# One transformer pair on one core: stick-breaking sums from rounded log rows and their rests, the output gate copied by ScalarE, few-row products placed among other products, and another bank pair for one query unit

## The chip, the core and the metric

The kernel runs on one core of one Trainium2 chip. The metric is the device time of one execution in microseconds (us), lower is better. The program is one stream of instructions for each engine: TensorE (PE, with its weight loads shown apart as PEld), VectorE (DVE), ScalarE (ACT), GpSimd (POOL) and SyncE (SP, which issues the loads). Engines meet only at semaphores that the kernel sets and waits on by hand.

## The reference, cut to what matters

Two blocks run one after the other on x of 256 tokens by 1024 features, all in float32. The first block mixes a stick-breaking attention (8 heads of 64) with a recurrent RWKV-7 layer (8 heads of 64), gates and adds them, and ends in a gated feed-forward part. The second block has dilated attention with a short convolution, a cross-attention to a memory of 256 rows, and a squared-ReLU feed-forward part. Two pieces of the first block bear on the change:

```
kk = k * k_k                                   # per head
kk = kk / max(norm(kk), 1e-12)                 # squares gathered over 64 features, root spread back
g  = sigmoid(xg) @ g_up                        # output gate of the recurrent layer
y  = groupnorm(scan) * lnx_w + lnx_b
out_rw = (y + bonus) * g                       # needs g * lnx_w and (bonus + lnx_b) * g

z  = q @ k.T                                   # stick-breaking attention, key j < query t
log_beta, log_rest = log_sigmoid(z), log_sigmoid(-z)
w[t, j] = exp(log_beta[t, j] + sum(log_rest[t, i] for j < i < t))
```

The sum over i is a product with a triangular matrix of ones, computed on TensorE on top of the logits in the same banks of PSUM.

## The kernel before, in words

All weights arrive in units of 1 MB (128 partitions by 2048 float32, names `raw`, `whi`, `wlo`), in a ring of three. SyncE loads a unit, ScalarE rounds it to float32r (`hi`, line 1289), VectorE subtracts to get the rest (`lo`, line 1762), and TensorE multiplies by activations that are split in the same way (`xhl`, rounded `xh` and rest `xl`). A product of float32r operands is one instruction; a product of plain float32 operands shows as two. A unit of 256 columns in `by_feature_wide` (line 519) is, for each of two tiles of 128 features, eight products of 512 columns by `whi` and eight of 256 columns by `wlo`; the function takes a hook `amidst(f, k)` that is called ahead of each product of 512 columns.

The order of the first block on TensorE is written by hand. Seven units `U_RW` (index 0 to 6) give the inputs of the recurrent layer, by `by_feature`; four units `U_QK` give queries and keys; two `U_V` give values; eight `U_G` give the gates. Placed among them:

- behind unit 4 of `U_RW` (line 664): the gather of squares `kq`, four products that give 8 rows (`kk_ss`). ScalarE takes the root (`krs`, `kk_sd`, line 1387); VectorE clips it and takes the reciprocal (lines 1850 and 1851, `kk_rs`), in its queue behind the evacuation of unit 5 and the rest `lo` of unit 8.
- behind the first unit of `U_QK` (line 680): the spread of `krs`, four products out of 8 rows (`kk_spread`), which wait for `kk_rs`.
- behind the first unit of `U_V` (line 689): the gate product with `gup` into banks 4 and 5 and the bonus sums into banks 6 and 7 (`bonus_mm`). VectorE reads all four banks (lines 1894 to 1905) and sets `gn_pre`. TensorE waits for `gn_pre` at line 851, before the stick-breaking logits of the first head pair overwrite banks 4 and 5.

Then a loop over four head pairs `p_` (line 862). Each turn: the logits into banks 4 and 5 (`sb_z`), a gate unit, the triangular sums (`sb_arg`), a second gate unit, the product with the values (`sb_o`). Inside and behind the gate units lie the small products of the recurrent layer (`before`, `amid`, `behind`): among them `join(i)`, which waits for VectorE's `Gm`, and, for the first pair, `before(1)`, which waits for VectorE's `Tm` (`pair_ready` 3). For a pair ScalarE makes `st1 = ln(1 + exp(-|z|))` in three steps, VectorE makes `st2` in two (lines 1970 and 1971, `sb_lf`), and the sums are float32 products of the constants `tri` (384 columns, two of them) and `ones` (128 columns, two) with `st2`. VectorE then makes `st3` (line 1978), ScalarE the exponential `st4`.

In the second block, lines 1067 to 1078 run four units `U_QK2`. Before them the memory's keys lie in banks 0 and 1 (`km`): ScalarE copies a half out, VectorE adds the other (line 1767, `summed`). Unit 0 uses bank 6, unit 1 uses banks 0 and 1 and so waits for that sum, unit 2 uses banks 6 and 7, unit 3 banks 0 and 1. After it comes a value unit in banks 2 and 3.

Of the kernel before, what the change touches and what calls it, by code (L numbers as in the profile page):

```python
# [6 lines left out]
P = 128  # L7
# [79 lines left out]
def block_kernel(nc, A, out, dbg=None):  # L87
# [9 lines left out]
    with ctx:  # L97
# [46 lines left out]
        st4 = at("st4", W + 91, [P, 2, 384])  # L144
        lora = at("lora", W + 94, [P, HW])
# [207 lines left out]
        QK2_BANKS = (None, (0, 1), (6, 7), (0, 1))  # L353
# [87 lines left out]
        def _(pe):  # L441
# [217 lines left out]

            for i, u in enumerate(U_RW):  # L660
                if i >= 3:
                    pe.wait_ge(sem("out_evac"), i - 2)
                by_feature(u, xh, xl, RW_BANK[i], None if i else "n1", amid_first(i))
                if i == 4:

                    pe.wait_ge(sem("kk_sq"), 1)
                    pe.wait_ge(sem("lora_evac"), 1)
                    pe.wait_ge(sem("cst_loaded"), 16)
                    for j in range(NPAIR):
                        last = mm(PS[0:NH, 4 * 512:4 * 512 + SEQ], C("gather")[:, NH * j:NH * (j + 1)], kq[:, j, :], j == 0,  # L670
                                  j == NPAIR - 1)
                    last.then_inc(sem("kk_ss"), 1)

            for i, u in enumerate(U_QK):
                if i == 1:
                    pe.wait_ge(sem("out_evac"), 7)
                elif i >= 2:
                    pe.wait_ge(sem("summed"), halved("qk", i - 1))
                by_feature_wide(u, xhl, QK_BANKS[i % 2])
                if i == 0:  # L680

                    pe.wait_ge(sem("kk_rs"), 1)
                    for j in range(NPAIR):
                        last = mm(PS[:, 4 * 512 + j * SEQ:4 * 512 + (j + 1) * SEQ], C("spread")[0:NH, j * P:(j + 1) * P], krs[:],
                                  True, True)
                    last.then_inc(sem("kk_spread"), 1)
# [113 lines left out]
            def amid(i):  # L800
# [13 lines left out]
                else:  # L814
                    pe.wait_ge(sem("chunk_ready"), 3)
                    tokens(eN, 0, "tok_T")
                    pe.wait_ge(sem("sb_arg_read"), NPAIR)
# [33 lines left out]
            pe.wait_ge(sem("gn_pre"), 1)  # L851
            def gate_unit(i):
# [9 lines left out]
            for p_ in range(NPAIR):  # L862

                if p_ == 0:
                    pe.wait_ge(sem("out_evac"), 11)
                else:
                    pe.wait_ge(sem("sb_arg_read"), p_)
# [5 lines left out]
                last.then_inc(sem("sb_z"), 1)  # L873
# [10 lines left out]
                pe.wait_ge(sem("sb_w"), p_ + 1)  # L884
# [9 lines left out]
                last.then_inc(sem("sb_o"), 1)  # L894
# [172 lines left out]
            for i, u in enumerate(U_QK2):  # L1067
# [4 lines left out]
                if i == 1:  # L1072
                    pe.wait_ge(sem("summed"), halved("km", 2))
                elif i == 2:
                    pe.wait_ge(sem("out2_evac"), 1)
                else:
                    pe.wait_ge(sem("summed"), halved("qk2", 1))
                by_feature_wide(u, xhl, QK2_BANKS[i])
            by_token(U_V2[0], xh, xl, 0, 2, True, False)

            def dilated_logits(p_):
# [3 lines left out]
                else:  # L1085
                    pe.wait_ge(sem("d_z_read"), p_)
# [4 lines left out]
                last.then_inc(sem("d_z"), 1)  # L1091
# [11 lines left out]
            def dilated_values(p_):  # L1103
# [7 lines left out]
                last.then_inc(sem("d_o"), 1)  # L1111
# [155 lines left out]
        def _(act):  # L1267
# [126 lines left out]
            A_(eX[:], sg[:], ACT.Exp, scale=-c0).then_inc(sem("decays"), 1)  # L1394
            for i, u in enumerate(U_QK):
# [3 lines left out]
            hi(U_V[0] + RING)  # L1399
            after(U_V[1])  # L1400
# [26 lines left out]
            for p_ in range(NPAIR):  # L1427
                act.wait_ge(sem("sb_z"), p_ + 1)
# [7 lines left out]
                if p_:  # L1436
                    hi(U_G[2 * p_ - 1] + RING)
                if p_:
# [9 lines left out]
                act.wait_ge(sem("sb_arg_read"), p_ + 1)  # L1448
                if p_:
                    act.wait_ge(sem("sb_o"), p_)  # L1450
                A_(st4[:], st3[:], ACT.Exp).then_inc(sem("sb_w"), 1)
# [12 lines left out]
            act.wait_ge(sem("sb_o"), NPAIR)  # L1464
# [120 lines left out]
            def dilated_exp(p_):  # L1585
# [5 lines left out]
                last.then_inc(sem("d_p"), 1)  # L1591
# [16 lines left out]
            for p_ in range(NPAIR):  # L1608
# [7 lines left out]
                if p_:  # L1616
                    act.wait_ge(sem("d_o"), p_)
# [14 lines left out]
            act.wait_ge(sem("d_o"), NPAIR)  # L1632
# [114 lines left out]
        def _(dve):  # L1747
# [147 lines left out]
            dve.wait_ge(sem("rw_pre"), 1)  # L1895
            for j in range(NPAIR):
                V.tensor_scalar(rw[:, j, :], PS[:, 4 * 512 + j * SEQ:4 * 512 + (j + 1) * SEQ], par_col("lnx_w", j), None, ALU.mult)
# [3 lines left out]
            link(last)  # L1901
            for j in range(NPAIR):
                last = V.scalar_tensor_tensor(out=rw[:, 4 + j, :], in0=bon[:, j, :], scalar=par_col("lnx_b", j),
                                              in1=PS[:, 4 * 512 + j * SEQ:4 * 512 + (j + 1) * SEQ], op0=ALU.add, op1=ALU.mult)
            last.then_inc(sem("gn_pre"), 1)
# [37 lines left out]
            def gate_unit(i):  # L1943
# [19 lines left out]
            for p_ in range(NPAIR):  # L1963
# [7 lines left out]
                V.tensor_tensor(st2[:], st2[:], M("sb_neg").unsqueeze(1).broadcast_to([P, 2, 384]), ALU.mult).then_inc(sem("sb_lf"), 1)  # L1971
# [4 lines left out]
                if p_:  # L1976
                    dve.wait_ge(sem("sb_w"), p_)
# [441 lines left out]
```

## Time and profile before

| | us |
|---|---|
| median of 3 runs | 841.4 (840.96 to 841.78) |
| the profiled execution | 841.16 |
| its span, first to last instruction | 839.4 |
| around the span | 1.8 |

| engine | busy us | share of the span | instructions |
|---|---|---|---|
| PE | 824.6 | 98% | 6332 |
| PEld | 715.2 | 85% | 6332 |
| DVE | 586.9 | 70% | 693 |
| ACT | 430.8 | 51% | 529 |
| POOL | 6.4 | 1% | 8 |

The mean granted clock of TensorE is 0.997 of full speed. The profile has several views. The page sums up one execution. The waits list who waited for whom. The timeline gives instructions of one engine in order of time; a row can merge several alike. A row's length reaches to the end of the last result, while the next product has already begun, so what a product costs is read from the starts of rows that follow each other. The windows give busy time and granted clock of a stretch. The groups by form give the count and cost of instructions of one shape.

### The profile page before, as it was taken

The page shows a single profiled execution, that of the slowest core. Times are in us where ns is not written, and L with a number is a line of the kernel's source. Part 1 is how long each engine was busy: PE and PEld are TensorE (multiplying, and loading weights), DVE is VectorE, ACT ScalarE, POOL GpSimd, SP SyncE. Part 2 cuts the span into 40 slices and gives each one's busy share as a digit, 9 for nine tenths or more (in the row PEclk, how much of TensorE's full clock was granted, in tenths as well). Part 3 has the DMA queues.
Part 4 walks back from the last instruction along what each step waited for, and adds up shares of the span by engine and source line. Part 5 has one row for each costly group of instructions (what it writes and reads, how often), then busy time and mean ns, then how long its engine had stood idle before and what let it go on. Part 6 is the DMA issues. An engine that isn't in the chain of part 4 may idle for free.

```text
span 839.4 us, 14921 instructions
## 1 busy us (share of the span) xinstructions
PE 824.6 (98%) x6332; PEld 715.2 (85%) x6332; DVE 586.9 (70%) x693; ACT 430.8 (51%) x529; POOL 6.4 (1%) x8
## 2 busy tenths in 40 slices
PE   9999999999999999999998999999999999999997
PEld 9998788888989888888887888888888888888885
DVE  5999865656887666656678567795764866676664
ACT  6644344474387544544466365546654544444443
POOL 0000010000000000000000000000000000000000
PEclk9999999999999999999999999999999999999999
DMA  9845513331764555565545553546423365555541
GB/s 301 289 152 177 175 53 102 103 102 52 280 209 159 180 201 185 165 216 185 200 157 177 168 194 108 192 143 201 167 100 126 133 228 182 180 180 183 192 149 50
DMA packets 96999, 140.55 MB, mean 167 GB/s; under 512 B 2480, under 2 KB 79408, under 8 KB 96944
## 3 DMA queue, kind: packets, MB, share of 16 engines
q1 hardware_dynamic: 96512, 139.36, 49.7%
q8 instruction: 43, 0.70, 0.3%
q10 hardware_dynamic: 432, 0.39, 0.2%
q14 instruction: 12, 0.10, 0.0%
HBM read 138.69 MB, written 1.05 MB: 166 GB/s over the span
## 4 chain that ended last, share of the span: by engine, by line
PE 83%; DVE 10%; ACT 3%; issue 3%; DMA 1%; POOL 0%; ACTq 0%; DVEq 0%; POOLq 0%
PE PS L443 81%; DVE wlo L1762 3%; ACT whi L1271 1%; PE PS L569 1%; DMA raw<-in_w_in_dram 1%; ACT st L1271 1%; DVE rw L1828 1%; ACT xhl L1271 1%; DVE diff L1825 1%; DVE stg L1823 1%; PE PS L1100 0%; DVE cs L1845 0%; PE PS L716 0%; DVE xhl L1789 0%; DVE TT L1924 0%
## 5 line engine op out<-in xcount | busy, mean ns | idle before, releaser
L1762 DVE TENSOR_TENSOR wlo<-raw,whi 128x2048 fp32r<-128x2048 f32 x122 | 278.2, 2289 | 78.7 <-ACT whi L1271 78.5
L443 PE MATMUL PS<-xhl,whi 128*128 128x512 f32 (+1 forms) x1328 | 308.5, 365 | 3.9 <-DVE km L1767 2.9
L1271 ACT ACTIVATE whi<-raw 128x2048 fp32r<-128x2048 f32 (+1 forms) x130 | 241.3, 1859 | 93.6 <-PE PS L443 90.1
L443 PEld LDWEIGHTS PS<-xhl,whi 128*128 128x128 f32 x1328 | 230.3, 190 | 40.3 <-DVE km L1767 3.1
L443 PE MATMUL PS<-xhl,wlo 128*128 128x256 f32 x1136 | 180.3, 282 | 0.1
L443 PEld LDWEIGHTS PS<-xhl,wlo 128*128 128x128 f32 x1136 | 163.7, 191 | 9.7 <-DVE wlo L1803 0.3
L443 PE MATMUL PS<-whi,fh 128*128 128x512 f32 x216 | 84.3, 391 | 0.0
L443 PE MATMUL PS<-wlo,fh 128*128 128x512 f32 x216 | 84.3, 390 | 0.0
L443 PE MATMUL PS<-whi,fl 128*128 128x512 f32 x216 | 84.0, 389 | 0.0
L1767 DVE TENSOR_TENSOR fa<-PS,fa 128x512 f32<-128x512 f32 x25 | 17.3, 691 | 62.7 <-ACT fa L1271 62.7
L443 PEld LDWEIGHTS PS<-whi,fl 128*128 128x128 f32 x216 | 40.6, 188 | 8.6
L443 PEld LDWEIGHTS PS<-whi,fh 128*128 128x128 f32 x216 | 40.7, 188 | 7.8
L443 PEld LDWEIGHTS PS<-wlo,fh 128*128 128x128 f32 x216 | 40.7, 188 | 7.5
L1271 ACT ACTIVATE fa<-PS 128x512 f32<-128x512 f32 x25 | 14.7, 589 | 52.4 <-PE PS L443 52.4
L1789 DVE SCALAR_TENSOR_TENSOR xhl<-PS,par,xhl 128x256 fp32r<-128x256 f32 x40 | 16.7, 476 | 11.7 <-ACT xhl L1271 11.7
L1271 ACT ACTIVATE fh<-fa 128x512 fp32r<-128x512 f32 x16 | 10.1, 633 | 25.9 <-DVE fa L2357 25.9
L1271 ACT ACTIVATE xhl<-PS,par 128x256 fp32r<-128x256 f32 x40 | 15.7, 481 | 12.1 <-PE PS L569 12.1
L443 PE MATMUL PS<-whi,memhl 128*128 128x512 f32 x64 | 20.7, 397 | 0.1
L443 PE MATMUL PS<-whi,xhl 128*128 128x512 f32 x64 | 20.7, 394 | 0.0
L1271 ACT ACTIVATE fh<-fb 128x512 fp32r<-128x512 f32 x11 | 7.0, 632 | 24.9 <-DVE fb L2173 24.9
L1271 ACT ACTIVATE gates<-PS 128x512 f32<-128x512 f32 x8 | 4.8, 597 | 27.9 <-PE PS L443 27.9
L1271 ACT ACTIVATE junk<-xres 128x1024 f32<-128x1024 f32 (+1 forms) x14 | 13.2, 945 | 9.9 <-DVE xres L2116 8.7
(327 smaller groups left out, 1035.3 us busy)
## 6 DMA issues: line engine op xcount, KB each, us to landing
raw<-in_w_in_dram SPq DMA_DIRECT2D x32, 1024.0 KB, 5.3
raw<-in_w_up_dram SPq DMA_DIRECT2D x16, 1024.0 KB, 5.3
raw<-in_w_down_dram SPq DMA_DIRECT2D x16, 1024.0 KB, 5.1
raw<-in_w_ffn_gate_dram SPq DMA_DIRECT2D x11, 1024.0 KB, 5.3
raw<-in_w_ffn_up_dram SPq DMA_DIRECT2D x11, 1024.0 KB, 5.3
raw<-in_w_ffn_down_dram SPq DMA_DIRECT2D x11, 1024.0 KB, 5.6
raw<-in_w_kv_mem_dram SPq DMA_DIRECT2D x8, 1024.0 KB, 5.3
raw<-in_w_o_dram SPq DMA_DIRECT2D x4, 1024.0 KB, 8.2
```

Source lines behind the costliest of these rows:

```text
L443: return nc.tensor.matmul(o, l, r, start=start, stop=stop, **kw)
L569: last = nc.tensor.transpose(PS[:, o:o + P], src[:, t, f * P:(f + 1) * P], C("ident"))
L1271: return nc.scalar.activation(o, i, f, **kw)
L1762: V.tensor_tensor(wlo[u % RING][:], raw[u % RING][:], whi[u % RING][:].bitcast(f32), ALU.subtract) \
L1767: return V.tensor_tensor(dst, tiles(banks)[:, :, 0], dst, ALU.add)
L1789: V.scalar_tensor_tensor(out=lo_[:, f0 + f, :], in0=PS[:, b * 512 + c * SEQ:b * 512 + (c + 1) * SEQ], scalar=par_col(g, f), in1=hi_[:, f0 ...
L1823: V.tensor_tensor(s[:, :, 1:SEQ + 1], two(RW_BANK[i]), spread(rs1[:]), ALU.mult).then_inc(sem("out_evac"), 1)
L1825: link(V.tensor_tensor(diff[:], s[:, :, 0:SEQ], s[:, :, 1:SEQ + 1], ALU.subtract))
L1828: last = V.scalar_tensor_tensor(out=rw[:, r, :], in0=diff[:, f, :], scalar=par_col("mu_rw", r), in1=s[:, f, 1:SEQ + 1], op0=ALU.mult, op1= ...
```

## The change

Five edits:

- Triangular sums: `st2` (the masked log rows) is rounded to float32r by ScalarE (`lfh`, in the place of `st3`), VectorE takes the rest (`lfl`, in the place of `st2`), and the sums are float32r products of rounded `tri_r` and `ones_r` with both parts. VectorE's subtraction stands in `gate_unit` behind `lower_out`, ahead of the wait for the gate's second half. `tri_r` and `ones_r` are made once by ScalarE.
- Output gate: ScalarE copies banks 4 and 5 out, once scaled by `lnx_w`, once plain into `rw[:, 4:8]` (`g_read`), and VectorE's product with the gate reads that. TensorE waits for `gn_pre`, now set behind VectorE's read of banks 6 and 7, and for `g_read`.
- The four gather products stand one by one in unit 5 of `U_RW`, two steps of `k` apart; the four spread products one by one in unit 0 of `U_QK`, at `k` of 2 and 6 of either tile. The wait for `kk_rs` goes with the first of them.
- Unit 1 of `U_QK2` uses banks 2 and 3; the wait for the sum of the memory's keys goes to unit 3, and the value unit waits for the sum of unit 1.
- Semaphores of the two attention parts are shared (`logits`, `logits_read`, `pair_weights`, `pair_values`), with counts carried on.

```diff
-        QK2_BANKS = (None, (0, 1), (6, 7), (0, 1))
+        QK2_BANKS = (None, (2, 3), (6, 7), (0, 1))
...
+            def gather_squares(f, k):
+
+                if f or k % 2:
+                    return
+                j = k // 2
+                if j == 0:
+                    pe.wait_ge(sem("kk_sq"), 1)
+                    pe.wait_ge(sem("lora_evac"), 1)
+                    pe.wait_ge(sem("cst_loaded"), 16)
+                last = mm(PS[0:NH, 4 * 512:4 * 512 + SEQ], C("gather")[:, NH * j:NH * (j + 1)], kq[:, j, :], j == 0, j == NPAIR - 1)
+                if j == NPAIR - 1:
+                    last.then_inc(sem("kk_ss"), 1)
+
+            def spread_norms(f, k):
+
+                if k not in (2, 6):
+                    return
+                j = 2 * f + k // 4
+                if j == 0:
+                    pe.wait_ge(sem("kk_rs"), 1)
+                last = mm(PS[:, 4 * 512 + j * SEQ:4 * 512 + (j + 1) * SEQ], C("spread")[0:NH, j * P:(j + 1) * P], krs[:], True, True)
+                if j == NPAIR - 1:
+                    last.then_inc(sem("kk_spread"), 1)
...
-                by_feature(u, xh, xl, RW_BANK[i], None if i else "n1", amid_first(i))
+                by_feature(u, xh, xl, RW_BANK[i], None if i else "n1", amid_first(i), 0, gather_squares if i == 5 else None)
...
-                by_feature_wide(u, xhl, QK_BANKS[i % 2])
+                by_feature_wide(u, xhl, QK_BANKS[i % 2], amidst=None if i else spread_norms)
...
             pe.wait_ge(sem("gn_pre"), 1)
+            pe.wait_ge(sem("g_read"), 1)
...
-                for e in range(2):
-                    mm(PS[:, (4 + e) * 512:(4 + e) * 512 + 384], C("tri"), st2[:, e, :], False, False, skip_group_check=True)
-                for e in range(2):
-                    last = mm(PS[:, (4 + e) * 512 + P:(4 + e) * 512 + SEQ], C("ones"), st2[:, e, SEQ:384], False, True, skip_group_check=True)
+                for part in (lfh, lfl):
+                    for e in range(2):
+                        mm(PS[:, (4 + e) * 512:(4 + e) * 512 + 384], tri_r[:], part[:, e, :], False, False, skip_group_check=True)
+                for part in (lfh, lfl):
+                    for e in range(2):
+                        last = mm(PS[:, (4 + e) * 512 + P:(4 + e) * 512 + SEQ], ones_r[:], part[:, e, SEQ:384], False, part is lfl,
+                                  skip_group_check=True)
...
-                if i == 1:
-                    pe.wait_ge(sem("summed"), halved("km", 2))
-                elif i == 2:
-                    pe.wait_ge(sem("out2_evac"), 1)
-                else:
-                    pe.wait_ge(sem("summed"), halved("qk2", 1))
+                if i == 2:
+                    pe.wait_ge(sem("out2_evac"), 1)
+                elif i == 3:
+                    pe.wait_ge(sem("summed"), halved("km", 2))
                 by_feature_wide(u, xhl, QK2_BANKS[i])
+            pe.wait_ge(sem("summed"), halved("qk2", 1))
             by_token(U_V2[0], xh, xl, 0, 2, True, False)
...
+            act.wait_ge(sem("bonus_mm"), 1)
+            act.wait_ge(sem("rw_pre"), 1)
+            for j in range(NPAIR):
+                A_(rw[:, j, :], PS[:, 4 * 512 + j * SEQ:4 * 512 + (j + 1) * SEQ], ACT.Copy, scale=par_col("lnx_w", j))
+            for j in range(2):
+                last = A_(rw[:, 4 + 2 * j:6 + 2 * j, :], bank(4 + j).rearrange("p (j t) -> p j t", j=2), ACT.Copy)
+            last.then_inc(sem("g_read"), 1)
...
+                act.wait_ge(sem("sb_masked"), p_ + 1)
+                A_(lfh[:], st2[:], ACT.Copy).then_inc(sem("sb_hi"), 1)
...
+                if i % 2 == 0:
+                    dve.wait_ge(sem("sb_hi"), i // 2 + 1)
+                    dve.wait_ge(sem("sb_masked"), i // 2 + 1)
+                    V.tensor_tensor(lfl[:], st2[:], lfh[:].bitcast(f32), ALU.subtract).then_inc(sem("sb_lf"), 1)
```

## Rows read from the trace of the kernel before

**Rows 1.** The page: busy time of each engine.

```profile
PE 824.6 (98%) x6332; PEld 715.2 (85%) x6332; DVE 586.9 (70%) x693; ACT 430.8 (51%) x529; POOL 6.4 (1%) x8
```

**Rows 2.** The waits of PE: who, for whom, us in total, times, longest.

```profile
PE PS L443 <- DVE km L1767: 2.9, 1, 2.9
PE PS L443 <- DVE rw L1903: 1.8, 1, 1.8
...
PE PS L443 <- DVE sq L1767: 0.2, 1, 0.2
```

**Rows 3.** Timeline of PE, first unit of `U_QK`, the spread: start, length, shape, count.

```profile
53.21 2.00 PE L443 MATMUL PS<-xhl,whi 128*128 128x512 f32 x8
55.05 1.12 PE L443 MATMUL PS<-xhl,wlo 128*128 128x256 f32 x8
...
58.89 1.99 PE L443 MATMUL PS<-krs,cst 8*128 8x256 f32 x8
60.91 0.50 PE L443 MATMUL PS<-xhl,whi 128*128 128x512 f32 x1
```

**Rows 4.** Timeline of DVE in the same stretch.

```profile
53.21 2.28 DVE L1762 TENSOR_TENSOR wlo<-raw,whi 128x2048 fp32r<-128x2048 f32 x1
...
55.72 1.74 DVE L1851 RECIPROCAL krs<-krs 8x256 f32<-8x256 f32 x1
```

**Rows 5.** Timeline of PE, the gate and bonus products.

```profile
83.69 1.89 PE L443 MATMUL PS<-rw,gup 128*128 128x256 f32 x8
85.41 1.89 PE L443 MATMUL PS<-rkk,cst 128*128 128x256 f32 x8
```

**Rows 6.** Windows: length, busy of PE, PEld, DVE, ACT, POOL; granted clock, DMA.

```profile
92.70:94.50 1.80, 0.05 (x1) 0.00 (x0) 1.71 (x5) 1.65 (x1) 0.00 (x0) 1.00 1.09 346
...
457.80:458.70 0.90, 0.00 (x0) 0.00 (x0) 0.90 (x3) 0.22 (x1) 0.00 (x0) 0.97 1.02 398
458.70:461.70 3.00, 2.96 (x7) 2.38 (x8) 2.78 (x2) 0.00 (x0) 0.00 (x0) 0.50 0.83 243
```

**Rows 7.** Timeline of DVE, then of ACT, around the gate product's evacuation.

```profile
85.50 4.49 DVE L1762 TENSOR_TENSOR wlo<-raw,whi 128x2048 fp32r<-128x2048 f32 x2
91.48 1.28 DVE L1899 TENSOR_TENSOR bon<-PS,rw 128x512 f32<-128x512 f32 x2
92.85 1.91 ACT L1271 ACTIVATE whi<-raw 128x2048 fp32r<-128x2048 f32 x1 [7.00 <-PE PS L443]
```

**Rows 8.** Timeline of PE, then of DVE, first head pair.

```profile
104.46 2.00 PE L443 MATMUL PS<-st,cst 128*128 128x384 f32 x8
106.30 0.60 PE L716 MATMUL PS<-cst,eX 128*128 128x128 f32 x4
106.83 1.09 PE L443 MATMUL PS<-cst,eX 128*64 128x128 f32 x16
...
102.64 1.28 DVE L1912 TENSOR_TENSOR TT<-PS,msk 128x512 f32<-128x512 f32 x2
104.71 1.28 DVE L1912 TENSOR_TENSOR Tm<-PS,msk 128x512 f32<-128x512 f32 x2
```

**Rows 9.** Timeline of PE, then of DVE and ACT, second head pair.

```profile
128.49 1.90 PE L443 MATMUL PS<-st,cst 128*128 128x384 f32 x8
130.14 0.48 PE L443 MATMUL PS<-xhl,whi 128*128 128x512 f32 x1
...
126.13 0.74 DVE L1931 TENSOR_TENSOR Gm<-PS,msk 128x256 f32<-128x256 f32 x2
119.64 1.72 ACT L1271 ACTIVATE st<-st 128x768 f32<-128x768 f32 x2
```

**Rows 10.** Timeline of PE, second block, after unit 0 of `U_QK2`; then DVE.

```profile
458.74 3.63 PE L443 MATMUL PS<-xhl,whi 128*128 128x512 f32 x8 [2.94 <-DVE km L1767]
462.21 1.11 PE L443 MATMUL PS<-xhl,wlo 128*128 128x256 f32 x8
...
452.15 2.29 DVE L1762 TENSOR_TENSOR wlo<-raw,whi 128x2048 fp32r<-128x2048 f32 x1 [0.76 <-ACT whi L1271]
```

More of the change, by code:

```diff
@@ L662, in _ @@
                     pe.wait_ge(sem("out_evac"), i - 2)
-                by_feature(u, xh, xl, RW_BANK[i], None if i else "n1", amid_first(i))
[L664 to L672, printed above, removed]
+                by_feature(u, xh, xl, RW_BANK[i], None if i else "n1", amid_first(i), 0, gather_squares if i == 5 else None)
             for i, u in enumerate(U_QK):
@@ L678, in _ @@
                     pe.wait_ge(sem("summed"), halved("qk", i - 1))
-                by_feature_wide(u, xhl, QK_BANKS[i % 2])
[L680 to L686, printed above, removed]
+                by_feature_wide(u, xhl, QK_BANKS[i % 2], amidst=None if i else spread_norms)
             for i, u in enumerate(U_V):
@@ L893, in _ @@
                     last = mm(PS[half(e), ob + P:ob + SEQ], sv[:, 1, head(2 * p_ + e)], st4[:, e, SEQ:384], False, True, skip_group_check=True)
-                last.then_inc(sem("sb_o"), 1)
+                last.then_inc(sem("pair_values"), 1)
             def place(g):
@@ L1090, in dilated_logits @@
                     last = mm(PS[:, (4 + e) * 512 + P:(4 + e) * 512 + 384], q2[half(e), p_, P:SEQ], k2[half(e), p_, :], True, True)
-                last.then_inc(sem("d_z"), 1)
+                last.then_inc(sem("logits"), 1)
             def dilated_turn(p_):
@@ L1110, in dilated_values @@
                     last = mm(PS[half(e), o + P:o + SEQ], v2[:, 1, head(2 * p_ + e)], dq[:, e, SEQ:384], False, True, skip_group_check=True)
-                last.then_inc(sem("d_o"), 1)
+                last.then_inc(sem("pair_values"), 1)
             def dilated_fill(i):
@@ L1427, in _ @@
             for p_ in range(NPAIR):
-                act.wait_ge(sem("sb_z"), p_ + 1)
+                act.wait_ge(sem("logits"), p_ + 1)
                 if p_:
@@ L1590, in dilated_exp @@
                                   accum_out=col(DL + 4 * p_ + 2 * t + e))
-                last.then_inc(sem("d_p"), 1)
+                last.then_inc(sem("pair_weights"), 1)
             def fill_tile(i, f):
@@ L1900, in _ @@
                                        rw[:, 8 + 2 * j:10 + 2 * j, :], ALU.mult)
-            link(last)
+            last.then_inc(sem("gn_pre"), 1)
+            dve.wait_ge(sem("gn_pre"), 1)
+            dve.wait_ge(sem("g_read"), 1)
             for j in range(NPAIR):
                 last = V.scalar_tensor_tensor(out=rw[:, 4 + j, :], in0=bon[:, j, :], scalar=par_col("lnx_b", j),
-                                              in1=PS[:, 4 * 512 + j * SEQ:4 * 512 + (j + 1) * SEQ], op0=ALU.add, op1=ALU.mult)
-            last.then_inc(sem("gn_pre"), 1)
+                                              in1=rw[:, 4 + j, :], op0=ALU.add, op1=ALU.mult)
+            link(last)
             lo(U_V[1] + RING)
@@ L2213, in dilated_max @@
                 z = PS[:, 4 * 512:6 * 512].rearrange("p (e n) -> p e n", e=2)[:, :, 0:384]
-                dve.wait_ge(sem("d_z"), p_ + 1)
+                dve.wait_ge(sem("logits"), NPAIR + p_ + 1)
                 if p_:
-                    dve.wait_ge(sem("d_p"), p_)
+                    dve.wait_ge(sem("pair_weights"), NPAIR + p_)
                 V.scalar_tensor_tensor(out=dz[:], in0=z, scalar=HD ** -0.5, in1=C("dil").unsqueeze(1).broadcast_to([P, 2, 384]),
-                                       op0=ALU.mult, op1=ALU.add).then_inc(sem("d_z_read"), 1)
-                dve.wait_ge(sem("d_z_read"), p_ + 1)
+                                       op0=ALU.mult, op1=ALU.add).then_inc(sem("logits_read"), 1)
+                dve.wait_ge(sem("logits_read"), NPAIR + p_ + 1)
                 for t, r in enumerate((slice(0, P), slice(P, 384))):
```

40 lines of the change are left out of this document (22 added, 18 removed).

## The prediction

> **What bounds the kernel now.** I read the page first: TensorE is busy in 98% of the span, VectorE in 70%, ScalarE in 51% [rows 1]. So time is won or lost where TensorE does less, stands still or runs slower. The waits of PE come next, since they say how little standing still there is: the longest are 2.9 us for the sum of the memory's keys, 1.8 us for the last product of the gate's evacuation, and 0.2 us for the first query sum [rows 2]. The change goes at the first two. The reader should then open the timelines of PE and of DVE side by side at each edit. From 53 to 58 us VectorE works without a gap [rows 4], while TensorE runs ahead of it; whatever makes TensorE ask for a VectorE result earlier there turns this lead into a wait. The windows with the granted clock come last. They show one fall: TensorE stands for 2.9 us until 458.74, and from 458.70 on it is granted 0.50 of full speed, its level of 1.2 GHz, before it is back at 2.4 GHz. The stand of 1.8 us before 94.50 was followed by no fall [rows 6].
>
> **Second block, banks 2 and 3 for unit 1.** The wait of 2.9 us falls away [rows 10]. Its eight products of 512 columns took 3.47 us (458.74 to 462.21) where the same eight take 1.84 us at full clock (53.21 to 55.05) [rows 3, 10], so the fall cost 1.63 us, and it goes with the stand that came before it. What is late next? Unit 1's rest was made from 452.15 to 454.4, before TensorE is free at 455.8 [rows 10]. The sum that unit 3 now waits for was ready at 458.7, and unit 3 starts two units of 5.6 us later. The value unit waits for a sum that is more than ten us old. Gain 4.6 us; bounds 4.2 and 4.8.
>
> **The spread, moved forward.** This is the term that speaks against the change. Before, the spread began at 58.89, behind the whole unit [rows 3], and nothing was waited for. Now its first product, and with it the wait for `kk_rs`, stands behind two products of 512 columns of that unit, which begins at 53.21: 2 x 0.23 = 0.46 us in, so at 53.7. The reciprocal ends at 55.72 + 1.74 = 57.46 [rows 4]. VectorE has no gap ahead of it and loses no work there, so it comes no sooner. All of TensorE's queue stands behind this wait. The gather, placed apart in a unit before, makes TensorE some 0.6 us later; that falls into the stand and costs nothing, but without it the stand is 3.8 us instead of 3.2. From 57.5 on the rest of the unit runs, 5.6 - 0.46 = 5.13 us, and with it the spread. Together in one run the spread takes 2.0 us (58.89 to 60.91) [rows 3]. A run of the same size with full weights takes 1.72 us (83.69 to 85.41) [rows 5]; the difference of 0.3 us is what going into and out of a product of 8 rows costs. Four such goings in place of one would add 0.9 us, nothing at the least (1.7 in all), 1.4 at the most. I take 2.9 us, nearest to the rows of this very product. So the next unit starts at 57.5 + 5.13 + 2.9 = 65.5 where it started at 60.91 [rows 3]: 4.6 us later (3.4 to 5.1). Two waits behind it are absorbed, the 0.2 us and the 1.8 us [rows 2]. Left: +2.6 us (1.4 to 3.1).
>
> Rule and row agree here in direction, and the rule goes against this edit. The Trainium skill, "TensorEngine Tiling (Array Packing)", section Key Properties, says that changing the tiling mode drains the engine; by it each of the four goings pays, and this sum would be at its upper end, 0.5 us more. Whether a product of 8 rows is another mode here, no row says.
>
> **The clock behind that stand.** TensorE stands for 3.2 to 3.8 us, longer than the 2.9 us after which the clock fell, and nearly twice the 1.8 us after which it did not [rows 6, 10]. I take it that the clock falls again and costs what it cost there: 1.6 us (0 if it does not fall, 1.7 at most).
>
> **The output gate by ScalarE.** VectorE is at `lo` until 85.50 + 4.49 = 89.99, then its two products `bon` take 1.3 us, so `gn_pre` is set at 91.3 instead of 94.5 [rows 7]. ScalarE stood idle for 7.0 us before 92.85 [rows 7]; six copies of no more than 0.86 us each, the price of a 768-column copy [rows 9], are 5.2 us at most and begin when the bonus sums end, at 85.41 + 1.72 = 87.1 [rows 5]. `g_read` is then there before TensorE ends the value unit at 92.7, and that order stays when TensorE is 4.6 us late. This removes the 1.8 us, which is already taken off above. VectorE's other products with the gate come later and delay only a rest that waits for ScalarE anyway.
>
> **Triangular sums.** Before, a pair's sums take 1.84 us (104.46 to 106.30) and 1.65 us (128.49 to 130.14), 1.75 us in the mean [rows 8, 9]. After, they are eight instructions of float32r: four of 384 columns and four of 128. One of 512 columns takes 0.23 us; one of 256 takes (58.89 - 53.21 - 16 x 0.23) / 16 = 0.12 us [rows 3]; so 384 take 0.175, four 0.70 us. No float32r product of 128 columns is in the trace. The low bound is half of 0.12; the high bound is all that a float32 product of 128 columns costs, two instructions of 0.13 us (106.30 to 106.83 for four) [rows 8]. I take one instruction of that, 0.13, the nearest in shape: 0.5 us. That is 1.2 us a pair (0.95 to 1.75), a gain of 0.55 us.
>
> ScalarE's rounding of `st2` adds 0.86 us [rows 9] and VectorE's rest 0.95 us a pair. In the second pair VectorE ends `Gm` at 126.87 and would end the rest at 127.8; TensorE wants it at 128.49 [rows 9]. It is covered with 0.7 us to spare, and the later pairs have the same order. In the first pair it is not: `TT` ends at 103.9 [rows 8], the rest at 104.9, and TensorE wants it at 104.46. Queued behind it on VectorE are the gate's sum (0.65 us) and `Tm` (1.25 us), which TensorE needs next. So `Tm` ends at 106.8, where TensorE was free at 106.30 [rows 8]: +0.5 us in the first pair, its gain swallowed (0.3 to 1.0). Three pairs gain 3 x 0.55 = 1.7 us (0 to 2.4). The two rounded constants cost ScalarE about half a us while TensorE stands. The shared semaphores keep the order of the waits and cost nothing.
>
> **The sum.** 2.6 + 1.6 + 0.5 - 1.7 - 4.6 = -1.6 us on the profiled execution of 841.16, which is 839.6 us. That execution is 0.24 us below the median of 841.4, too little to shift it. Elsewhere TensorE is without waits worth naming [rows 2], so a us that it gains or loses arrives at the end.
>
> **Rivals.**
> - The clock does not fall in the stand. For it: the one fall came when TensorE had stood for 2.9 us, little less than here, and one case makes no law. Against: this stand is longer. The 1.6 us go: 838.0 us.
> - The short float32r products are slow or the rests come late, so the pairs give nothing: 839.6 + 1.7 = 841.3 us. For it: no row has such a product, and the cover of the rest is 0.7 us. Against: the wide float32r products are paid by the column.
> - Slower: the clock stays low after the stand, because the spread's products, which use 8 of 128 rows, stand among the others for the whole unit. Work left in that unit is 8.0 us; at half the clock throughout it costs 8.0 instead of 1.6 us more, so 839.6 + 6.4 = 846.0 us. It decides the sign once the low clock costs over 1.6 + 1.8 + 1.7 = 5.1 us. Against: after 458.70 full clock was back in some three us [rows 6], and the spread run of before saw no fall. The Trainium skill, "TensorE: Matmul & The Clock Gate", section What's actually happening, calls the throttled level the default and says activity releases it; how a product of 8 rows counts as activity it does not say.
> - The change does not do what it says: the stand does not arise because `kk_rs` comes at 53.7. It would need VectorE to skip 3.8 us of queue; nothing does that. It would give 839.6 - 1.6 - 3.2 = 834.8 us.
>
> **How the numbers follow.** Chances: forecast 0.50, no fall 0.28, pairs give nothing 0.12, slower 0.07, no stand 0.03. The forecast's own range, from its bounds, is 838.2 to 841.0. The range of 8 in 10 takes in the no-fall case with the pairs and the second block at their good bounds (836.6) and the pairs giving nothing (841.3). About 0.2%, 1.7 us, is what a measurement of this kernel can tell from no change, so faster means below 839.7. The forecast falls there in a bit over half its cases (0.27), the no-fall case nearly always (0.27), the last one too (0.03): 0.57. Slower means above 843.1: 0.07 and a rest of mishaps, 0.08. The same: 0.35.
>
> **What would show it.** In the profile of after: a wait of PE for `krs` (line of the reciprocal) of 3.2 to 3.8 us near 57.5, and a granted clock of 0.50 behind it; no wait for `km`, and full clock in the second block; no wait at the first logits; sums of a pair within 1.2 us; a short wait of PE for `Tm` in the first pair. I am wrong by 3 us if the stand is not there, by 1.6 if the clock stays up, by up to 1.7 if a pair's sums take as long as before.

## The result, and the profile after

| | before | after |
|---|---|---|
| median, us | 841.35 (6 runs, 840.96 to 841.78) | 844.95 (6 runs, 840.75 to 845.68) |
| profiled execution, us | 841.16 | 845.28 |
| its span, us | 839.4 | 843.5 |
| mean granted clock in it | 0.997 | 0.989 |

The ratio is 1.0037, with a 95% interval of 1.0023 to 1.005: slower by 0.4%, where 839.6 was forecast and 841.3 was the upper end of the range. The executions of the changed kernel mostly fall in two groups, near 841 and near 845.4, and the mean granted clock goes with them (0.994 and 0.989), so below a time is read beside its clock. By 843 us times a difference in mean clock one gets roughly the time that the clock took: 0.005 is 4 us. It is rough because a low clock behind TensorE's last product costs nothing: in a kernel below (the spread back in its old place) such a tail of 2.9 us is nearly all that is missing from 1.00, and the mean is 0.998.

The page of the changed kernel. Its first row answers to [rows 1]; the second is TensorE's granted clock in 40 slices of 21 us, in tenths.

```profile
PE 830.3 (98%) x6332; PEld 718.2 (85%) x6332; DVE 588.6 (70%) x693; ACT 436.9 (52%) x541; POOL 7.0 (1%) x8
PEclk9987999999999999999999999999999999999999
```

TensorE has as many instructions as before and is busy 5.7 us longer. The clock row says where to look: the third and fourth slices, 42 to 84 us.

The waits of PE in the changed kernel, as in [rows 2].

```profile
PE PS L448 <- DVE krs L1879: 2.7, 1, 2.7
...
PE PS L729 <- DVE Tm L1940: 0.4, 1, 0.4
...
PE PS L448 <- DVE lfl L1984: 0.3, 1, 0.3
```

The two long waits of before are gone, `km` and the last product of the gate's evacuation. One of 2.7 us has come for the reciprocal, and two short ones in the first head pair.

The timeline of PE in the changed kernel, first unit of `U_QK` with the spread in it (start, length, operation, shape, count, idle time before), as in [rows 3].

```profile
54.14 0.63 PE L448 MATMUL PS<-xhl,whi 128*128 128x512 f32 x2
57.49 1.22 PE L448 MATMUL PS<-krs,cst 8*128 8x256 f32 x2 [2.72 <-DVE krs L1879]
58.63 2.08 PE L448 MATMUL PS<-xhl,whi 128*128 128x512 f32 x4
60.64 1.22 PE L448 MATMUL PS<-krs,cst 8*128 8x256 f32 x2
61.79 1.22 PE L448 MATMUL PS<-xhl,whi 128*128 128x512 f32 x2
...
65.50 1.22 PE L448 MATMUL PS<-krs,cst 8*128 8x256 f32 x2
...
68.65 1.22 PE L448 MATMUL PS<-krs,cst 8*128 8x256 f32 x2
...
72.53 2.95 PE L448 MATMUL PS<-xhl,whi 128*128 128x512 f32 x8
```

The windows of the changed kernel over the same stretch (length; busy of PE, PEld, DVE, ACT, POOL; granted clock; DMA).

```profile
53.00:57.50 4.50, 1.78 (x14) 1.35 (x13) 4.46 (x5) 3.08 (x2) 0.00 (x0) 1.00 0.18 25
57.50:72.00 14.50, 14.50 (x36) 9.17 (x37) 8.55 (x17) 3.46 (x6) 0.00 (x0) 0.50 0.38 137
72.00:74.00 2.00, 2.00 (x8) 1.71 (x8) 0.60 (x1) 1.23 (x2) 0.00 (x0) 0.50 0.00 0
74.00:76.00 2.00, 2.00 (x12) 1.72 (x11) 1.58 (x3) 1.17 (x1) 0.00 (x0) 0.86 0.04 8
```

Four products of 512 columns take 2.01 us (58.63 to 60.64) where they take 0.92 us at full clock. The clock is at 0.50, its level of 1.2 GHz, from 57.5 until about 74.5: of the last window 28% is still low. That is 17 us, over the whole rest of this unit and the start of the next. The next unit begins at 72.53 instead of 60.91 [rows 3].

The other edits, in the changed kernel. The timeline of PE at the sums of the first and the second head pair, as in [rows 8, 9].

```profile
115.04 0.62 PE L448 MATMUL PS<-lfh,tri_r 128*128 128x384 f32 x2 [0.32 <-DVE lfl L1984]
...
116.84 0.66 PE L729 MATMUL PS<-cst,eX 128*128 128x128 f32 x4 [0.42 <-DVE Tm L1940]
...
139.00 0.60 PE L448 MATMUL PS<-lfh,tri_r 128*128 128x384 f32 x2
...
139.79 0.33 PE L448 MATMUL PS<-lfh,ones_r 128*128 128x128 f32 x2
139.96 0.39 PE L448 MATMUL PS<-lfl,ones_r 128*128 128x128 f32 x2
140.19 1.14 PE L448 MATMUL PS<-xhl,whi 128*128 128x512 f32 x4
```

The sums of the second pair take 1.19 us (139.00 to 140.19) where they took 1.65 [rows 9]. The first pair pays two waits, 0.32 and 0.42.

The timeline of ACT at the gate's copies, then of PE at the first logits.

```profile
99.35 1.57 ACT L1287 ACTIVATE rw<-PS,par 128x256 f32<-128x256 f32 x4 [1.48 <-PE PS L448]
100.80 1.10 ACT L1287 ACTIVATE rw<-PS 128x512 f32<-128x512 f32 x2
...
104.70 0.92 PE L448 MATMUL PS<-sq,sk 64*128 64x256 f32 x8
```

The six copies take 2.55 us and are done at 101.9, the logits start at 104.70 without a wait.

The timeline of PE in the second block, as in [rows 10], and then the window.

```profile
463.90 0.71 PE L448 MATMUL PS<-dg,one 128*128 128x128 f32 x4
464.36 2.10 PE L448 MATMUL PS<-xhl,whi 128*128 128x512 f32 x8
```

```profile
463.00:470.00 7.00, 6.97 (x44) 6.09 (x43) 6.20 (x8) 3.76 (x3) 0.00 (x0) 1.00 0.68 226
```

Unit 1 goes on without a stand, at full clock.

### The profile page after: what moved, and what is told of

Same layout as the page of the kernel before. It is cut to its first block, busy times and chain, and to the rows that moved or that the text cites. A ratio compares the mean times of both kernels' runs of the same rounds, so it can differ in the third digit from the quotient of the medians.

```text
span 843.5 us, 14939 instructions
## 1 busy us (share of the span) xinstructions
PE 830.3 (98%) x6332; PEld 718.2 (85%) x6332; DVE 588.6 (70%) x693; ACT 436.9 (52%) x541; POOL 7.0 (1%) x8
## 4 chain that ended last, share of the span: by engine, by line
PE 88%; DVE 6%; issue 3%; ACT 2%; DMA 1%; POOL 0%; ACTq 0%; DVEq 0%; POOLq 0%
PE PS L448 86%; PE PS L574 1%; DVE wlo L1790 1%; DMA raw<-in_w_in_dram 1%; ACT st L1287 1%; ACT whi L1287 1%; DVE rw L1856 1%; DVE diff L1853 0%; DVE stg L1851 0%; DVE st L2002 0%; DVE st L2003 0%; PE PS L1116 0%; PE PS L729 0%; DVE cs L1873 0%; ACT xhl L1287 0%
## 5 line engine op out<-in xcount | busy, mean ns | idle before, releaser
L448 PE MATMUL PS<-xhl,whi 128*128 128x512 f32 (+1 forms) x1328 | 312.2, 367 | 0.7 <-ACT xhl L1287 0.7
L2148 DVE TENSOR_TENSOR xres<-xres,PS 128x512 f32<-128x512 f32 x12 | 8.2, 687 | 13.7 <-PE PS L448 13.5
```

The lines of the kernel that those rows point to most:

```text
L448: return nc.tensor.matmul(o, l, r, start=start, stop=stop, **kw)
L2148: V.tensor_tensor(xres[:, t, h], xres[:, t, h], bank(b + 2 * t + c), ALU.add).then_inc(norm_sem(then, "x"), 1)
```

## The experiments

Theory A: what the changed kernel lost is the long low clock, and two things together make it: the stand for `kk_rs` in front of the unit, and the products of 8 rows that stand apart in the unit behind it. Theory B: the stand alone makes it. Theory C: it is not the 8 rows but the float32 products, any that break up the float32r stream. Diffs are against the changed kernel unless it is said otherwise.

### Is it the spread at all? The spread back in its old place

```diff
-                by_feature_wide(u, xhl, QK_BANKS[i % 2], amidst=None if i else spread_norms)
+                by_feature_wide(u, xhl, QK_BANKS[i % 2])
+                if i == 0:
+                    pe.wait_ge(sem("kk_rs"), 1)
...
+                        last = mm(PS[:, 4 * 512 + j * SEQ:4 * 512 + (j + 1) * SEQ], C("spread")[0:NH, j * P:(j + 1) * P], krs[:], True, True)
```

> The changed kernel with the spread as before, four products together behind the first query unit, with its wait there. All theories: no stand, no fall. From the working of the prediction, the rest of the change gives -1.8 (gate) + 0.5 (first pair) - 1.7 (other pairs) - 4.6 (second block) + 0.6 (gather apart) = -7.0 us on 841.4: 834.4. Against x3 it shows what apart costs by itself, 0.9 us expected.

Measured: 833.89 us, ratio 0.9917 (0.99 to 0.9933), clocks 0.996 to 0.999. The timeline of PE in this kernel:

```profile
59.84 1.99 PE L448 MATMUL PS<-krs,cst 8*128 8x256 f32 x8
61.76 2.12 PE L448 MATMUL PS<-xhl,whi 128*128 128x512 f32 x8
```

No wait, and the second unit starts at 61.76. So this one edit costs all of the loss and the gain of the four others besides: 11.6 us between the two profiled executions (845.28 and 833.7). The other edits bring 7.5 us, as the forecast's terms have it (4.6 + 1.8 + 1.7 - 0.5 = 7.6; with 0.6 for the gather apart, 7.0).

### The stand without products apart, and the products together

The wait stays in the unit. In the first kernel the four products follow in one run behind the unit, in the second they stand in one run right behind the wait.

```diff
                 if j == 0:
                     pe.wait_ge(sem("kk_rs"), 1)
-                last = mm(PS[:, 4 * 512 + j * SEQ:4 * 512 + (j + 1) * SEQ], C("spread")[0:NH, j * P:(j + 1) * P], krs[:], True, True)
...
+                if i == 0:
+                    for j in range(NPAIR):
+                        last = mm(PS[:, 4 * 512 + j * SEQ:4 * 512 + (j + 1) * SEQ], C("spread")[0:NH, j * P:(j + 1) * P], krs[:], True, True)
```

> The changed kernel, with the wait for kk_rs left inside the first query unit, but the four spread products together behind that unit. Theory A (the stand makes the clock fall, and the products of 8 rows that stand apart behind it hold it down): TensorE stands 2.7 us near 57.5, the clock is at 0.50 for some 3 us and back at 1.00 before 62; the time is the changed kernel's 845.0 less 6.3 us of low clock and less 0.9 us of going in and out, about 838. Rival B (a stand of this length alone brings a long low clock, whatever follows): 0.50 until about 73, about 844.

> The changed kernel with the four spread products in one run right behind the wait inside the unit. Theory A: the low clock lasts while these eight instructions run (3.4 us at half clock) and some 3 us of full products behind them, until about 64; some 3.3 us of low-clock cost, about 839 to 840. Rival B: 0.50 until about 73, about 844. Rival C (what holds the clock down is only that the products stand apart, not their rows): as A, but back at 61, about 838.

Measured: 837.44 us, ratio 0.9956 (0.994 to 0.9973), clocks 0.996 to 0.998, and 839.64 us, ratio 0.9973 (0.9964 to 0.9983), clocks 0.994 to 0.997. The timeline of PE in the first of them, and then its window:

```profile
57.56 1.66 PE L448 MATMUL PS<-xhl,whi 128*128 128x512 f32 x6 [2.73 <-DVE krs L1880]
...
62.89 1.99 PE L448 MATMUL PS<-krs,cst 8*128 8x256 f32 x8
```

```profile
57.50:60.00 2.50, 2.44 (x14) 2.18 (x15) 2.36 (x9) 0.17 (x1) 0.00 (x0) 1.00 0.97 372
```

The stand is the same 2.7 us and the clock stays up, so the stand alone does not bring the long low clock: theory B falls. Theory A had a fall of some 3 us here, and this execution has none; whether the two runs at 838.07 and 838.3 (clocks 0.997 and 0.996) have one is not known. Against the spread in its old place this profiled execution (836.75) is 3.1 us longer, which is the stand and little else. The windows of the second:

```profile
60.00:62.00 2.00, 2.00 (x8) 1.38 (x7) 1.93 (x6) 0.32 (x1) 0.00 (x0) 0.78 0.62 241
62.00:64.00 2.00, 2.00 (x8) 1.71 (x7) 1.93 (x5) 2.00 (x3) 0.00 (x0) 0.50 0.01 4
64.00:66.00 2.00, 2.00 (x12) 1.79 (x11) 2.00 (x2) 1.03 (x3) 0.00 (x0) 0.87 0.00 0
```

Here the clock fell, behind the run of 8-row products (58.84 to 60.76) and not behind the stand itself, for 0.88 + 2.0 + 0.52 = 3.4 us, and only full-row products followed. That cost 1.7 us. TensorE came to this unit at 55.48, 1.3 us later than in the changed kernel, for a delay in the first 20 us, so this execution's time is not the low clock alone.

### The products apart without the stand

The four products go apart into the second unit of `U_QK`, when the reciprocal is long there.

```diff
-                by_feature_wide(u, xhl, QK_BANKS[i % 2], amidst=None if i else spread_norms)
+                by_feature_wide(u, xhl, QK_BANKS[i % 2], amidst=spread_norms if i == 1 else None)
```

> The changed kernel with the spread apart in the same way, but in the second query unit, where kk_rs has long come: no stand. Theory A: no fall, clock 1.00 throughout, only 0.9 us for going in and out: 835. Rival D (products of few rows among others bring the clock down by themselves): 0.50 from about 60 until the unit is over, 840 or more.

Measured: 836.61 us, ratio 0.9949 (0.9933 to 0.9965), clocks 0.998 and 0.999 in four runs and 0.994 in one (839.38 us). Its timeline of PE:

```profile
61.37 0.73 PE L448 MATMUL PS<-xhl,whi 128*128 128x512 f32 x2 [1.02 <-DVE stg L1851]
62.04 0.69 PE L448 MATMUL PS<-krs,cst 8*128 8x256 f32 x2
62.66 1.20 PE L448 MATMUL PS<-xhl,whi 128*128 128x512 f32 x4
...
70.39 2.00 PE L448 MATMUL PS<-xhl,whi 128*128 128x512 f32 x8
```

The unit with the spread in it takes 9.02 us (61.37 to 70.39). A unit takes 5.6 and the spread in one run 1.92 (59.84 to 61.76 above), 7.5 in sum: the products apart cost 1.5 us at full clock, so three goings more cost 0.5 each, not 0.3. A wait of 1.0 us for an evacuation comes to it, since the spread no longer covers it. With this wait in place of the stand of 2.7 us, the clock fell by the mean in one run of five and in no window of the profiled one.

### Rows or float32?

Both kernels keep the wait and the real spread in one run behind the unit, and put other products at its four places; their results are not used. In the first these are float32 products over all 128 rows, in the second float32r products of 8 rows, two at each place.

```diff
-                last = mm(PS[:, 4 * 512 + j * SEQ:4 * 512 + (j + 1) * SEQ], C("spread")[0:NH, j * P:(j + 1) * P], krs[:], True, True)
+                mm(PS[:, 4 * 512 + j * SEQ:4 * 512 + (j + 1) * SEQ], C("blockones"), kq[:, j, :], True, True)
```

```diff
+                for _ in range(2):
+                    mm(PS[:, 4 * 512 + j * SEQ:4 * 512 + (j + 1) * SEQ], whi[U_QK[0] % RING][0:NH, 0:P], xh[0:NH, j, :], True, True)
```

> The changed kernel with its stand, but what stands apart in the unit behind it are four float32 products of the same size that use all 128 rows (their results are overwritten unused); the real spread runs together behind the unit. It adds 1.7 us of products to the kernel with the spread behind the stand's unit, which took 837.4. Theory A (the 8 rows hold the clock down, full rows do not): 839.2, clock 0.50 for 4 us at the most. Rival C (any float32 products apart among the others hold it down): 0.50 until the unit is over, near 70, 845 or more.

> The changed kernel with its stand, but what stands apart are eight float32r products of 256 columns that use 8 rows (results unused); the real spread runs together behind the unit. One such instruction streams as many columns as one of the two instructions of a float32 product, at half the time. Theory A: the rows hold the clock down, though for half the time: 0.50 well beyond 62, 841 to 845. Rival C (what counts is float32, in two passes): no fall or one of 3 us, 839 at the most.

Measured: 841.44 us, ratio 1.0002 (0.9993 to 1.0012), clocks 0.995 to 0.998, and 849.33 us, ratio 1.0059 (1.003 to 1.0088), with six runs at 849.2 to 849.9 (clocks 0.986 and 0.987) and four at 841.7 to 843.4 (0.995 to 0.997). The windows of the kernel with full rows, and then a row of its PE timeline:

```profile
57.50:60.00 2.50, 2.33 (x6) 1.86 (x7) 2.36 (x9) 0.29 (x1) 0.00 (x0) 0.51 0.99 374
60.00:62.00 2.00, 2.00 (x10) 1.71 (x9) 1.93 (x4) 1.49 (x2) 0.00 (x0) 0.76 0.05 18
62.00:64.00 2.00, 2.00 (x13) 1.77 (x13) 2.00 (x3) 1.87 (x4) 0.00 (x0) 1.00 0.00 0
```

```profile
169.93 0.27 PE L448 MATMUL PS<-v_tok,AK 64*64 64x64 f32 x2 [1.34 <-issue]
```

The windows of the kernel with float32r products of 8 rows:

```profile
57.50:58.70 1.20, 1.16 (x5) 0.93 (x6) 1.13 (x4) 0.16 (x1) 0.00 (x0) 0.99 0.99 372
58.70:66.00 7.30, 7.30 (x22) 5.06 (x21) 7.16 (x14) 3.35 (x5) 0.00 (x0) 0.50 0.22 76
66.00:76.00 10.00, 10.00 (x27) 7.20 (x26) 5.04 (x5) 2.40 (x2) 0.00 (x0) 0.50 0.31 104
76.00:80.00 4.00, 4.00 (x16) 3.48 (x16) 0.10 (x1) 0.00 (x0) 0.00 (x0) 0.60 0.84 262
```

With full rows the clock fell behind the same stand and was back at 61, after 3.4 us and with two of the four products still to come. With 8 rows it stayed low for some 20 us. The first 11.4 of them (58.7 to 70.1) are this unit, in which no float32 product stood; then the real spread ran, at the low clock too. So theory C falls: of rows and float32 it is the rows. The two kernels also differ in the number of the products and in their data, which no run separates. Not every run has the long fall (a mean clock of 0.989 or less): 7 of 16 of the changed kernel (845.07 to 845.68) and 6 of 10 of this one, against none of the 14 runs in which only full-row products stood in that unit (4 with the spread behind it, 10 here). Both kernels came out later than forecast. In both, TensorE has a stop of 1.3 us (near 170 and 178 us) that the profile ascribes to nothing; the changed kernel has none. They have 16 instructions more in all (14955 for 14939), but that this is its cause is not shown.

### A shorter stand, with all else as changed

VectorE clips and takes the reciprocal ahead of the rest `lo` of unit 8, in its loop over the units of `U_RW`.

```diff
-                if i != 2:
+                if i != 2 and i != 5:
...
+                    lo(u + RING)
```

> The changed kernel with VectorE's clip and reciprocal of the root ahead of the rest of unit 8 instead of behind it: kk_rs at 55.3 instead of 57.5, so the stand shrinks from 2.7 to about 0.7 us while the spread stays apart in the first query unit. Theory A (stand and few rows have to come together): no fall, 833.9 + 1.4 (apart, as in the second query unit) + 0.7 = 836.0. Rival D (apart alone brings the clock down): 840 or more.

Measured: 835.56 us, ratio 0.9932 (0.9916 to 0.9949); clocks 0.998 and 0.999 in three runs, 0.996 in the profiled one (837.21). The stand is 0.74 us. Windows of the profiled one:

```profile
57.50:60.00 2.50, 2.50 (x9) 1.90 (x9) 2.40 (x8) 0.16 (x1) 0.00 (x0) 0.56 0.44 77
60.00:62.00 2.00, 2.00 (x9) 1.36 (x8) 1.90 (x5) 1.37 (x2) 0.00 (x0) 0.70 1.05 408
```

Even here the clock can fall, once, for 2.2 + 1.2 = 3.4 us. It is back by 61.2, before the third and the fourth of the products apart. With the stand cut by 2.0 us, most of the loss of the changed kernel is gone.

### The other edits, one by one

Added to the kernel before: the banks of the second block alone; the output gate alone; the triangular sums alone, with the shared semaphores. And the changed kernel with both the gather and the spread in their old places. The cores of the four edits, the first three against the kernel before:

```diff
-        QK2_BANKS = (None, (0, 1), (6, 7), (0, 1))
+        QK2_BANKS = (None, (2, 3), (6, 7), (0, 1))
```

```diff
             pe.wait_ge(sem("gn_pre"), 1)
+            pe.wait_ge(sem("g_read"), 1)
```

```diff
-                    mm(PS[:, (4 + e) * 512:(4 + e) * 512 + 384], C("tri"), st2[:, e, :], False, False, skip_group_check=True)
+                for part in (lfh, lfl):
+                    for e in range(2):
+                        mm(PS[:, (4 + e) * 512:(4 + e) * 512 + 384], tri_r[:], part[:, e, :], False, False, skip_group_check=True)
```

```diff
-                by_feature(u, xh, xl, RW_BANK[i], None if i else "n1", amid_first(i), 0, gather_squares if i == 5 else None)
-                by_feature_wide(u, xhl, QK_BANKS[i % 2], amidst=None if i else spread_norms)
+                by_feature(u, xh, xl, RW_BANK[i], None if i else "n1", amid_first(i))
+                by_feature_wide(u, xhl, QK_BANKS[i % 2])
```

> The kernel before with the other bank pair for unit 1 of the second block's queries alone. Theory: the wait of 2.9 us goes and with it the low clock of 1.6 us behind it: -4.6 us, 836.9. Rival (the wait moves to unit 3, to the value unit or to a rest): -2 us or less.

> The kernel before with the output gate copied by ScalarE alone. Theory: the wait of 1.8 us at the first logits goes and nothing takes its place, since VectorE's chain of the first pair ends early enough: -1.8 us, 839.7. Rival (the chain from the values' copies on ScalarE is what the first pair waits for then): 841.4.

> The kernel before with the triangular sums in float32r alone (the attention parts' semaphores shared as in the change). Theory: +0.5 us in the first pair, -0.55 us in each of three others: -1.2 us, 840.3. Rival (the sums' gain is eaten by later waits of PE for the rests): 841.4 or more.

> The changed kernel with gather and spread both as before, in one run each behind their units. Theory (going in and out of few-row products costs, and nothing is won by setting them apart): 0.6 us less than with the gather apart, which took 833.9: 833.3. Rival (the gather apart is free or better): 833.9 or more.

| kernel | us | ratio (95%) | clocks |
|---|---|---|---|
| banks alone | 837.18 | 0.9947 (0.9933 to 0.9961) | 0.996 to 0.998 |
| gate alone | 840.75 | 0.9988 (0.9979 to 0.9996) | 0.992 to 0.997 |
| sums alone | 840.29 | 0.9983 (0.9974 to 0.9991) | 0.994 to 0.999 |
| gather and spread back | 834.42 | 0.9913 (0.9899 to 0.9928) | 0.996 to 0.998 |

The gate alone brought 0.6 us in the median where 1.8 were expected. Its profiled execution (841.64) has more low clock than that of before, in two places. The timeline of PE in the second block and the window behind it:

```profile
458.12 3.78 PE L443 MATMUL PS<-xhl,whi 128*128 128x512 f32 x8 [2.94 <-DVE km L1775]
...
463.41 2.23 PE L443 MATMUL PS<-xhl,whi 128*128 128x512 f32 x8
```

```profile
458.10:463.60 5.50, 5.48 (x17) 4.70 (x18) 2.76 (x2) 0.00 (x0) 0.00 (x0) 0.50 0.92 280
```

The wait at the logits is gone, but the clock fell within the untouched stand for `km` (0.54 from 457.0 to 458.1) and stayed low for 5.8 us behind it, where it was low for some 3 us before [rows 6]. The second place is behind the spread, which has no wait in front of it here. The timeline of PE there and then the window, with the window of the sums alone as the last row:

```profile
59.02 1.99 PE L443 MATMUL PS<-krs,cst 8*128 8x256 f32 x8
60.95 3.64 PE L443 MATMUL PS<-xhl,whi 128*128 128x512 f32 x8
```

```profile
60.00:70.00 10.00, 10.00 (x45) 8.22 (x44) 9.89 (x14) 6.83 (x7) 0.00 (x0) 0.83 0.34 109
...
60.00:70.00 10.00, 10.00 (x46) 8.27 (x45) 9.89 (x14) 7.31 (x9) 0.00 (x0) 0.83 0.34 108
```

In both the clock was at 0.50 for 3.4 us of this stretch. So a run of four 8-row products can be followed by a fall with no stand near it. In the profiled executions of the kernel before, of the banks alone and of the two kernels with the spread back, the same run of products was followed by full clock.

In its two runs whose clock is 0.997, that of before, the gate alone took 839.43 and 839.75 us: 1.6 to 1.9 less, as expected; these are two runs of eleven, picked by their clock. The sums alone lie between 838.61 us (0.999) and 841.57 us (0.994), so their 1.1 us rests on the clock as well; the interval of the ratio makes it 0.8 to 2.2. The gather together in place of apart makes 0.5 us more (834.42 against 833.89), no more than the runs differ, where 0.6 less was expected; by the timelines the unit behind it starts 0.7 us sooner (53.45 against 54.17), which later waits take back.

### The changed kernel once more

> The changed kernel itself, on the same chip as the three others, for the spread of its clock from run to run. All theories: near 845, a few runs lower where the fall comes late or ends early.

Measured: 842.46 us, ratio 1.0017 (1.0 to 1.0035). Five of ten runs were between 840.7 and 841.3 (clocks 0.994 and 0.995), four between 845.0 and 845.6 (0.987 to 0.989), one at 843.67 (0.991). Windows of the one at 845.07:

```profile
53.00:57.50 4.50, 1.84 (x14) 1.41 (x12) 4.47 (x5) 3.01 (x2) 0.00 (x0) 0.93 0.13 19
57.50:72.00 14.50, 14.43 (x36) 9.11 (x37) 8.64 (x18) 3.54 (x6) 0.00 (x0) 0.50 0.39 139
```

Here the clock fell already within the stand, before any product of 8 rows. It is the same program each time; what differs is when and for how long the clock is low. That the changed kernel is slower at all hangs on this too: here the interval of the ratio begins at 1.0, and half the runs take no more than the kernel before (841.4).

## Why the prediction was wrong

**The step that failed is "The clock behind that stand".** That the clock falls behind this stand was right and the size was not: I took 1.6 us, the price of the one fall in the trace of before [rows 6, 10]. Measured are 7.7 us: from 57.49 to 72.53 the rest of the unit takes 15.04 us, where the same products take 8.35 us at full clock (62.04 to 70.39, the products apart without the stand), which makes 6.7; and 2.0 us of the next unit ran at half the clock, 1.0 more. The price of before came from one fall behind a stand with only full-row products after it, and even there it is no constant: the same stand was followed by 5.8 us of low clock in the gate alone. Here products of 8 rows followed at 57.5, 60.6, 65.5 and 68.7, and the clock came back only 4.8 us after the last of them had ended (69.8 to 74.5). That such products act like stands that repeat is my reading. What is shown is that, behind the same stand, full-row products in their places let the clock return after 3.4 us and 8-row products, in half of the runs, do not.

**The rival that had it** is the third, "the clock stays low after the stand": 846.0 us by its working, with 8.0 us for the low clock; the runs near 845.4 are that case, with 7.7. I gave it 0.07, with two arguments against. That full clock was back in three us [rows 6] speaks of a unit without such products, and that the spread of before saw no fall speaks of a run without a stand in front of it, in one execution: in the profiles of the gate alone and of the sums alone the clock fell behind that very run. Neither row shows both conditions together; with nothing in the trace that covers a condition, 0.07 was too sure. "Slower" got 0.08 for that reason alone. The Trainium skill, "TensorE: Matmul & The Clock Gate", section What's actually happening, calls the throttled level the default and says activity releases it. The trace shows that level but no release by a busy PE row: 1.2 GHz is held for 17 us while PE is busy in 14.50 of 14.50 us.

**Terms that held, and by how much.** The table sets the forecast beside the measurement, as time that the edit adds.

| term | forecast | measured | from |
|---|---|---|---|
| stand for `kk_rs` | 3.2 with the gather apart | 2.72 | timeline after |
| goings into 8-row products | 0.9 (0 to 1.4) | 1.5 | products apart without the stand |
| low clock | 1.6 (0 to 1.7) | 7.7 (3 to 4 in the runs near 841) | timeline and windows after |
| banks of the second block | -4.6 (4.2 to 4.8) | -4.2 | banks alone |
| output gate | -1.8 | -1.6 to -1.9 at the same clock | gate alone |
| sums, all four pairs | -1.2 | -1.1 (-0.8 to -2.2) | sums alone |

The goings were nearer to the upper end of my range than to my value: 1.5 us measured, 1.4 at the most. The rule of the Trainium skill, "TensorEngine Tiling (Array Packing)", section Key Properties, that changing the tiling mode drains the engine, had pointed to that end. Whether it is that mechanism no run here shows. The stand was 0.5 us shorter since TensorE came to the unit at 54.14, 0.3 us later than 53.21 and the 0.6 us of the gather would have it, and its two first products end 0.63 us in, not 0.46. The wait for `Tm` came as forecast (0.42); the wait of 0.32 for the rest `lfl` in front of the first sums did not stand in the sum by itself.

Against the profiled runs the account closes: the spread moved costs 2.7 + 1.5 + 6.7 + 1.0 = 11.9 us by these rows and 11.6 by the two executions. The forecast had 2.6 + 1.6 and the 2.0 us of absorbed waits, 6.2. The difference of 5.4 to 5.7 is the miss (845.28 against 839.6).

**"No stand"** (0.03) and **"the pairs give nothing"** (0.12) are out. **"No fall"** (0.28) would have given 838.0; by the measured terms it is 833.9 + 2.7 + 1.5 = 838.1. None of the 16 runs of the changed kernel took under 840.7 us or had a mean clock above 0.995, so the clock most likely fell in all of them, for shorter or longer. The runs near 841 have some 3 us of it by that sum, 843 x 0.005 = 4 us by the clock.

**What stays open:** why one run of the same program has 3 to 4 us and another 8 us of it. The moment of the fall differs from kernel to kernel and from run to run (within the stand, right behind it, 1.2 us later, and some 2 us later), but no profile of a run near 841 was taken.

**The better kernel.** The changed kernel with the spread in its old place takes 833.89 us, 0.9917 of the time before (0.99 to 0.9933), and 1.3% less than the changed kernel (844.95).

## What to carry to other kernels

Before a small product is moved into a dense stream, look at who makes its operand and when: a wait that stood behind a unit's work is free, the same wait in the middle of the unit was 2.7 us here. Price a stand of TensorE with what follows it: with products of 8 rows scattered behind this one the clock was at 1.2 GHz for 17 us, which cost 7.7 us, three times the stand itself. Keep few-row products together, and far from any stand; even so a run of them was followed by 3.4 us of low clock in two profiles. Take the price of a low clock from several executions, since one trace shows one draw; and read the granted clock beside the busy share, since a TensorE that is 100% busy can be at half its speed.

## What the runs showed that I had not expected

- Behind the same stand and with PE busy throughout, the clock was low for 17 us with 8-row products scattered (changed kernel) and about 20 us (float32r of 8 rows), against 3.4 us with full rows at the same places. The long fall came in half of the runs of the two kernels with 8 rows.
- No stand is needed for a short fall: behind the run of four 8-row products in its old place the clock was low for 3.4 us in two profiles, and not in four others.
- The clock can fall away from a long stand: behind 0.74 us of standing and products of 8 rows it fell some 2 us later, and a stand of 2.73 us with full-row products behind it saw no fall in the profiled run.
- Going from 128-row to 8-row float32 products and back costs 0.5 us each time at full clock.
- Float32r products of 128 columns cost 0.10 us each (139.79 to 140.19 for four), less than half of float32's 0.26 us for one of that shape.
